# The first layer's shift on TensorE, and v's weights split ahead of h's parts, in a four-layer float32 kernel

## The reference

```
c_act = silu(c)                                   # (1, 1024)
mod = c_act @ w_mod[0] + b_mod[0]                 # (1, 6 * 1024)
sh_a, sc_a, gt_a, sh_f, sc_f, gt_f = split(mod, 6)
h = rmsnorm(x, g_mix_pre[0]) * (1 + sc_a) + sh_a  # (1, 256, 1024)
qkv = h @ w_qkv[0]                                # v first, then q and k
```

## Time and profile before

| what | value |
|---|---|
| median of 3 runs | 1455.71 us (1454.94 to 1458.83) |
| the profiled execution | 1458.6 us, span of its core 1457.4 us |
| PE busy | 1347.1 us, 92% of the span |
| DVE busy | 1051.8 us, 72% |
| ACT busy | 741.6 us, 51% |
| read from memory | 313.32 MB |

### The profile page before, as it was taken

The page is one execution under the profiler, slowest core; times in us unless marked ns, Lnnn a source line. Parts: engine busy times, 40 slices in busy tenths (PEclk is TensorE's granted clock), DMA queues, the critical chain, the costliest instruction groups (busy, mean ns, idle before and its releaser), DMA issues.

```text
span 1457.4 us, 22183 instructions
## 1 busy us (share of the span) xinstructions
PE 1347.1 (92%) x8848; PEld 1206.4 (83%) x8848; DVE 1051.8 (72%) x1628; ACT 741.6 (51%) x1241; POOL 104.3 (7%) x146
## 2 busy tenths in 40 slices
PE   4899899999899989999858999889999999899999
PEld 3798799987688779997646777579998899799987
DVE  6777788887648778789755675767878697666643
ACT  3665755543746575453634555564444454644441
POOL 0012000000004100000022241200000000000000
PEclk9999999999999999999988999989999999999999
DMA  8865467779467534667730512338788657356550
GB/s 339 333 231 209 167 241 257 283 310 340 146 218 272 200 119 174 242 249 279 272 141 30 202 58 109 123 118 306 297 316 309 243 218 273 127 221 238 224 202 29
DMA packets 46758, 315.81 MB, mean 217 GB/s; under 512 B 5168, under 2 KB 7744, under 8 KB 9280
## 3 DMA queue, kind: packets, MB, share of 16 engines
q1 hardware_dynamic: 46656, 314.40, 57.4%
HBM read 313.32 MB, written 1.06 MB: 216 GB/s over the span
## 4 chain that ended last, share of the span: by engine, by line
PE 64%; DVE 16%; ACT 7%; DMA 6%; issue 4%; POOL 2%; SPq 1%; DVEq 0%; ACTq 0%; POOLq 0%
PE mat L578 13%; PE mat L580 13%; PE mat L579 13%; DVE wlo L1470 6%; PE mat L617 5%; PE mat L619 5%; PE mat L621 5%; DVE raw L1488 3%; ACT whi L1038 3%; DMA raw<-in_down 2%; DMA raw<-in_mod 1%; POOL st L2058 1%; PE mat L930 1%; ACT tmp L1061 1%; DMA raw<-in_qkv 1%
## 5 line engine op out<-in xcount | busy, mean ns | idle before, releaser
L1470 DVE TENSOR_TENSOR wlo<-raw,whi 128x1024 fp32r<-128x1024 f32 x393 | 475.9, 1227 | 195.3 <-ACT whi L1038 194.1
L578 PE MATMUL mat<-hHL,whi 128*128 128x256 f32 x1864 | 534.0, 287 | 7.4 <-DVE tmp L1691 3.3
L579 PE MATMUL mat<-hHL,whi 128*128 128x256 f32 x1864 | 530.1, 284 | 0.0
L580 PE MATMUL mat<-hHL,wlo 128*128 128x256 f32 x1864 | 529.9, 284 | 0.0
L1038 ACT ACTIVATE whi<-raw 128x1024 fp32r<-128x1024 f32 x393 | 405.7, 1052 | 229.2 <-DMA raw<-in_down 75.9
L578 PEld LDWEIGHTS mat<-hHL,whi 128*128 128x128 f32 x1864 | 359.4, 193 | 14.1 <-issue 5.3
L579 PEld LDWEIGHTS mat<-hHL,whi 128*128 128x128 f32 x1864 | 359.5, 193 | 0.1
L580 PEld LDWEIGHTS mat<-hHL,wlo 128*128 128x128 f32 x1864 | 359.2, 193 | 0.0
L1488 DVE SCALAR_TENSOR_TENSOR raw<-raw,cB 128x1024 f32<-128x1024 f32 x192 | 233.9, 1229 | 13.7 <-DMA raw<-in_mod 13.5
L617 PE MATMUL mat<-whi,aHL 128*128 128x512 f32 x352 | 114.1, 394 | 2.1 <-DVE wlo L1470 2.0
L619 PE MATMUL mat<-wlo,aHL 128*128 128x512 f32 x352 | 112.9, 391 | 0.0
(11 more groups left out here) (207 smaller groups left out, 1539.4 us busy)
## 6 DMA issues: line engine op xcount, KB each, us to landing
raw<-in_mod SPq DMA_DIRECT2D x96, 1024.0 KB, 5.6
raw<-in_qkv SPq DMA_DIRECT2D x48, 1024.0 KB, 7.0
raw<-in_gate SPq DMA_DIRECT2D x44, 1024.0 KB, 5.0
raw<-in_up SPq DMA_DIRECT2D x44, 1024.0 KB, 5.3
raw<-in_down SPq DMA_DIRECT2D x44, 1024.0 KB, 5.8
raw<-in_wo SPq DMA_DIRECT2D x16, 1024.0 KB, 4.9
cB<-in_crow SPq DMA_DIRECT2D x3, 512.0 KB, 8.6
x<-in_x SPq DMA_DIRECT2D x1, 1024.0 KB, 8.9
```

Source lines behind the costliest of these rows:

```text
L578: pe.matmul(o, wh[:, k, :], hH[:, k, :], start=(k == 0), stop=False)
L579: pe.matmul(o, wh[:, k, :], hL[:, k, :], start=False, stop=False)
L580: m = pe.matmul(o, wl[:, k, :], hH[:, k, :], start=False, stop=(k == KT - 1))
L1470: dve.tensor_tensor(out=wlo[:, n % NSPL, :], in0=raw[:, f % NRAW, 1024 * h:1024 * h + 1024], in1=whi[:, n % NSPL, :].bitcast(f32), op=ALU. ...
```

## The change

Three quarters of the shift (q = 1 to 3) leave DVE. Their weights are laid out on the host with the summed index on the partitions, and `silu(c)` is also kept as a column of 128 partitions x 8 (`ccol`); TensorE makes 16 products of one column each for a quarter, with the 128x128 weights as the loaded operand, plain float32, into bank 4 of PSUM (`start_shift(q)`). Quarter 1 is put before v's first product, quarter 2 after group 1 and quarter 3 after group 3. The fetch four places on now waits for these products (`s_shift`). In each round ACT splits both halves of v's weights (`hi(2)`) before it makes h, and DVE both (`lo(2)`) before the two pieces of `hL`. The column's `silu` is put on ACT between the two squares of x.

```diff
-STEPS_FIRST = [(0, p, j) for q in range(4) for p in (1, 0) for j in (2 * q, 2 * q + 1)]
+STEPS_FIRST = [(0, 1, 0), (0, 1, 1), (0, 0, 0), (0, 0, 1)] + [(0, 1, j) for j in range(2, 8)]
...
+                    if old[:3] == ("mod", 0, 0) and old[3] > 0:
+                        sp.wait_ge(s_shift, old[3])
...
+        def start_shift(q):
+            f = FETCH_OF["mod", 0, 0, q]
+            w = raw[:, f % NRAW, :].rearrange("p (k n) -> p k n", k=8)
+            if q == 1:
+                pe.wait_ge(s_ccol, 1)
+                pe.wait_ge(s_tma, 2)
+            else:
+                pe.wait_ge(s_mod, FIN_AT[0, 1, q - 1])
+            pe.wait_ge(s_raw[f % NRAW], 16 * (f // NRAW + 1))
+            for i in range(2):
+                for k in range(KT):
+                    m = pe.matmul(shift_tile(q)[:, i:i + 1], w[:, k, P * i:P * i + P], ccol[:, k:k + 1], start=(k == 0),
+                                  stop=(k == KT - 1))
+            m.then_inc(s_shift, 1)
...
+            start_shift(1)
...
-                          then={(0, 0): lambda: transposes(b, 0, 2, 3), (5, 0): lambda: by_tile_second(b)} if l else None)
+                          then={(0, 0): lambda: transposes(b, 0, 2, 3), (5, 0): lambda: by_tile_second(b)} if l else
+                          {(1, 1): lambda: start_shift(2), (3, 1): lambda: start_shift(3)})
...
+                if t == 0:
+                    act.wait_ge(s_small, 16)
+                    act.activation(ccol[:, :], sm[:, SM["c"][0]:SM["c"][0] + 8], ACT.Silu).then_inc(s_ccol, 1)
             act.wait_ge(s_tr, 2)
...
+            for q in range(4):
+                hi(2)
+                for k in (2 * q, 2 * q + 1):
+                    y = start_rows(k)
+                    if k % 2 == 0:
+                        act.wait_ge(s_mod, FIN_AT[0, 1, q])
...
+            if q:
+                dve.wait_ge(s_shift, q)
+            dve.tensor_tensor(out=modc[:, 0, at], in0=shift_tile(q) if q else modc[:, 0, at], in1=sm[:, b[0]:b[0] + 2], op=ALU.add).then_inc(s_mod, 1)
...
             for q in range(4):
-                for p, j in ((1, 2 * q), (1, 2 * q + 1), (0, 2 * q), (0, 2 * q + 1)):
-                    mod_step(0, p, j)
...
+                for j in (2 * q, 2 * q + 1):
+                    mod_step(0, 1, j)
...
                 start_columns(q)
+                lo(2)
                 for k in (2 * q, 2 * q + 1):
-                    lo(1)
```

More of the change, by code:

```diff
@@ L23, in _layout @@
             [(f"wc{l}{k}", FT) for l in range(2) for k in range(3)] + [(f"bc{l}", FT) for l in range(2)] + \
-            [(f"sc{k}", 8) for k in range(3)] + [("bf", 1)]:
+            [(f"sc{k}", 8) for k in range(3)] + [("bf", 1), ("c", 8)]:
         SM[name] = (at, n)
@@ L162, in _mod_counts @@
             if (l, p) in ((0, 0), (0, 1)):
-                if p == 0 and j % 2:
+                if p == 1 and j % 2:
                     FIN_AT[0, 1, j // 2] = 3 * (j // 2) + 3
@@ L237, in build @@
         sm = sb("sm", [P, NSM])
+        ccol = sb("ccol", [P, KT])
         modc = sb("modc", [P, 26, 8])
@@ L261, in build @@
             "s_half", "s_prod", "s_tile", "s_tr", "s_trc", "s_gate_row"))
-        s_mem, s_const, s_c = (sem(n) for n in ("s_mem", "s_const", "s_c"))
+        s_mem, s_const, s_c, s_ccol, s_shift = (sem(n) for n in ("s_mem", "s_const", "s_c", "s_ccol", "s_shift"))
         s_hi, s_lo, s_tma, s_tmd, s_hh, s_hl = (sem(n) for n in ("s_hi", "s_lo", "s_tma", "s_tmd", "s_hh", "s_hl"))
@@ L506, in sync_program @@
                     old = FETCHES[f - NRAW]
-                    if old[0] == "w":
+                    if old[:3] == ("mod", 0, 0) and old[3] > 0:
+                        sp.wait_ge(s_shift, old[3])
+                    elif old[0] == "w":
                         sp.wait_ge(s_lo, CHUNKS[old[1]][2][-1] + 1)
@@ L665, in start_tile, with shift_tile @@
             return bank(4 + k // 2)[:, 256 * (k % 2):256 * (k % 2) + 256]
+        def shift_tile(q):
+            return bank(4)[:, 2 * q:2 * q + 2]
+        def start_shift(q):
[12 more added lines that the diff above has]
+            m.then_inc(s_shift, 1)
         def tensor_program():
@@ L1168, in scalar_program @@
                 act.activation(xn[:, t, :], x[:, t, :], ACT.Square, accum_out=norm_sum(0, t, 1)).then_inc(s_sq, 1)
+                if t == 0:
+                    act.wait_ge(s_small, 16)
+                    act.activation(ccol[:, :], sm[:, SM["c"][0]:SM["c"][0] + 8], ACT.Silu).then_inc(s_ccol, 1)
             act.wait_ge(s_tr, 2)
[L1170 to L1178, removed]
+            for q in range(4):
[4 more added lines that the diff above has]
+                        act.wait_ge(s_mod, FIN_AT[0, 1, q])
+                    act.activation(y, start_tile(k), ACT.Identity, bias=modc[:, 0, k:k + 1], scale=modc[:, 1, k:k + 1]
+                                   ).then_inc(s_tma, 1)
+                    act.wait_ge(s_tma, k + 1)
+                    act.activation(hH[:, k, :], y, ACT.Copy).then_inc(s_hh, 1)
             for l in range(LAYERS):
@@ L1515, in start_columns @@
             b, g = ([SM[name][0] + 2 * q for name in names] for names in (("b00", "b01"), ("g0a",)))
-            dve.wait_ge(s_step, STEP_AT[0, 0, 2 * q + 1, 0])
-            dve.tensor_tensor(out=modc[:, 0, at], in0=modc[:, 0, at], in1=sm[:, b[0]:b[0] + 2], op=ALU.add).then_inc(s_mod, 1)
+            dve.wait_ge(s_step, STEP_AT[0, 1, 2 * q + 1, 0] if q else STEP_AT[0, 0, 1, 0])
             dve.tensor_tensor(out=modc[:, 1, at], in0=modc[:, 1, at], in1=sm[:, b[1]:b[1] + 2], op=ALU.add).then_inc(s_mod, 1)
-            dve.wait_ge(s_mod, 3 * q + 2)
+            dve.wait_ge(s_mod, 3 * q + 1)
             dve.scalar_tensor_tensor(out=modc[:, 1, at], in0=modc[:, 1, at], scalar=1.0, in1=sm[:, g[0]:g[0] + 2], op0=ALU.add,
                                      op1=ALU.mult).then_inc(s_mod, 1)
+            if q:
+                dve.wait_ge(s_shift, q)
+            dve.tensor_tensor(out=modc[:, 0, at], in0=shift_tile(q) if q else modc[:, 0, at], in1=sm[:, b[0]:b[0] + 2], op=ALU.add).then_inc(s_mod, 1)
         def head_mods(l, step):
@@ L1646, in vector_program @@
             for q in range(4):
-                for p, j in ((1, 2 * q), (1, 2 * q + 1), (0, 2 * q), (0, 2 * q + 1)):
-                    mod_step(0, p, j)
[L1649 to L1652, removed]
+                for j in (2 * q, 2 * q + 1):
+                    mod_step(0, 1, j)
+                if q == 0:
+                    for t in range(2):
+                        vector_start_scale(t)
+                    dve.wait_ge(s_small, 16)
+                    for j in range(2):
+                        mod_step(0, 0, j)
                 start_columns(q)
+                lo(2)
                 for k in (2 * q, 2 * q + 1):
-                    lo(1)
                     dve.wait_ge(s_hh, k + 1)
@@ L2103 @@
         arrays[f"mod{l}"] = np.concatenate([tok(mod[:, 1024 * p:1024 * p + 1024].T) for p in range(6)])
+        if l == 0:
+            arrays["mod0"][1:4] = mod[:, 256:1024].reshape(8, P, 3, 256).transpose(2, 1, 0, 3).reshape(3, P, 2048)
         if b == 0:
@@ L2141 @@
     parts["bf"] = bf
+    parts["c"] = I["c"][0]
     arrays["smalls"] = np.ascontiguousarray(np.concatenate([cols(parts[n]) for n in SM], axis=1))
```

## The result

The changed kernel takes 1463.69 us (median of 5, 1462.62 to 1468.04) against 1455.67 us of the kernel before: a ratio of 1.0052, 95% interval 1.0036 to 1.0067. It is slower by 0.5%, where 1448.5 was forecast.

A forecast was written before the change was run, and what follows sets the result against it. TensorE was taken to bound most of the kernel, the start's v product running at DVE's pace; with the first q product 7.2 earlier, 1455.7 - 7.2 = 1448.5 us, range 1444.5 to 1455.

The forecast's parts named there:

- The start of the q product as the measure: What the first 58 us lose or gain, the end does; the first q product starts at 57.93 before the change.
- the removal on DVE: Six mod_steps leave DVE, 6.9 us; a round then takes 6.2 against 9.9 if nothing is waited for.
- hidden by 1 us: Fetch of the first TensorE shift's weights lands at 19 to 20, under the second h's end at 20.9.
- The later fetches: Weights for the second and third shifts land with margins of 1.3 and 2; if late, about 1451.
- The shift's products: One-column products on TensorE: 0.11 each at the high clock, 0.205 at the low; 16 cost 1.75 or 3.3.
- my own formula: v's queue on TensorE ends at 43.7 + 64c, c being one shift product at the high clock; 0.11 gives 50.7.
- the slower rival: Each of the 48 shift products is loaded and passed several times: c = 0.44, 1469.6, slower from c = 0.222; 5%.
- Load and product in turn: A shift product's load and pass on TensorE don't overlap: c 0.19 to 0.30, 1.2 slower, 1457; 13%.
- The clock falls again: Thin shifts count as pauses, low clock follows on TensorE: 3 to 6 of the 7.2 lost, about 1452.5; 12%.
- the 50.5 of the queue: Sum along TensorE's queue from the first shift to the first q product: 50.5 against 57.93, 7.4 less.
- The rule of the Trainium skill: Read as a plain float32 product passing TensorE's array four times: c would be 4 x 0.11.

The follow-up runs named there:

- experiment 3: The changed kernel with every second term of the shift's sums in quarters 1 to 3 left out, 8 products instead of 16 a quarter: 1452.72 us, ratio 0.9962.
- experiment 5: The kernel of experiment 4 with shift products on ready rounded operands, one load-and-pass pair each, so sums of other data: 1448.03 us, ratio 0.996 to the kernel before.
- experiment 4: The changed kernel with silu(c)'s column repeated 128 times in each shift product, same loads: 1454.86 us, ratio 0.9984 to the kernel before.
- experiment 1: The kernel before with only the splitting of v's weights put ahead on ScalarE and VectorE, the shift staying on VectorE: 1451.01 us, ratio 0.9955.
- experiment 7: The kernel before with only the splitting ahead, as in experiment 1, measured a second time: 1450.69 us, ratio 0.9966.

## Why the prediction was wrong

**What held.** The start of the q product as the measure held (table). So did the removal on DVE: its steps, splits and pieces took what they were put at, and it waited for TensorE, not the other way. The first shift began at 20.95, put at 20.9, but that is luck: the second h, which I had put at 20.9, was over at 20.29, and it was the fetch that ended the wait, landing at 20.82 where I had put it at 19 to 20 and called it hidden by 1 us. The later fetches cost nothing. ACT's new order cost nothing that shows.

**The step that failed: "The shift's products".** I put one at 0.11 at the high clock and 0.205 at the low. It took 3.46 / 16 = 0.22 and, from start to start, 6.82 / 16 = 0.43. The reading was of line 816, "of which two take 0.22": two rows of the trace, not two products of the program. Line 816 has 32 rows, and the program issues it once for each of 16 heads. A plain float32 product is two load-and-pass pairs here, each 0.11. The transposes have one row each, 16 for 16, so their 0.205 was a load's price and not a plain product's. Experiments 3 and 5 show both: half the products cost half, and one-pair products cost 1.75 for a shift. By my own formula c = 0.22 gives 43.7 + 14.1 = 57.8, which is no gain at all, and just the break-even that I had named for the slower rival. That rival had the mechanism, several loads for one product, at twice the price. "Load and product in turn" had a c of 0.19 to 0.30, and 0.22 lies in it, but its mechanism is not what happened: 128 columns cost no more than one (experiment 4), and a product of one pair takes 0.11 (experiment 5). (The middle of its ends, 55.9 and 62.9, is 59.4 and not 59.1; its 1457 stands.)

**The rival that came true beside it.** "The clock falls again" had 12% and 3 to 6 us of price. It fell at the end of the second shift and behind the third, and cost, against the terms of my sum, 2.95 in groups 2 and 3 (8.35 instead of 5.4) and 1.8 in the last four (12.6 instead of 10.8), 4.75 in all. Experiment 4 shows that the single column was the reason. The argument against it, that a shift of 1.75 is shorter than those pauses, hung on the wrong price: at 3.5 to 3.9 it is longer than the 2.5 that had let the clock fall before, and at 1.7, in experiment 3, it didn't fall. I had priced the rivals one at a time, and one made the other.

**The sum again, with the measured terms**, against the 50.5 of the queue: first shift +3.5 (6.8 instead of 3.3), groups 0 and 1 +0.5 (7.1 instead of 6.6), second shift +2.2 (3.9 instead of 1.75, of which 0.4 is the clock's), groups 2 and 3 +2.95, third shift +1.7, the last four groups +1.8: 12.7, which makes 63.2.

**The rule of the Trainium skill.** The Trainium skill, "TensorE: Matmul & The Clock Gate", section "Terms", says of the transpose mode that it is four times faster for float32. I had multiplied line 816's 0.11 by that four, and 0.11 is one row of two: hence 0.44 and 1469.6, where 0.22 was measured. Between the transposes and the plain products the rows show 0.205 against 0.43 at the low clock, a factor of 2.1, and the measurement decides. As I had read it, four passes for a plain product, the factor nearly shows with more columns. The kernel before has plain float32 products of 256 columns too, line 815, again two rows for one product, and products of rounded parts with 256 columns, line 578, one row each. Two pieces of its chain, and line 815's rows:

```profile
58.45 0.12 PE mat L578
...
91.81 0.43 PE mat L815 x2
...
L815 PE MATMUL mat<-att,tri_neg x32: 379/380/483, 80.1 to 148.0; 128*128 128x256 f32 x32
```

With 256 columns the plain product takes 0.43 against 0.12, 3.6 times as long. With one column or 128 it takes 0.22 against the 0.11 of one pair in experiment 5, twice as long.

**Where the forecast of the whole went astray.** The gain that I gave to both halves of the change together belongs to one. The splitting ahead alone brings the q product forward by 5.6. Taking the shift off DVE could add little: at the prices that I had forecast, with the clock's late rise (experiment 5), the first q product comes at 51.92, only 0.45 before the 52.37 of the splitting alone. At the real prices TensorE needs 21.6 for v's 96 products, and the three shifts of 3.5 to 6.8 in the same queue take 14.2 more.

**Open.** The medians are 8.0 apart where the q product's start says 5.3 and the spans 5.0. The interval (5.2 to 9.8 us) just holds 5.3; that executions of the kernel before differed by 12 us among themselves (1448.56 to 1460.94 in one comparison) may be all of it, and was not followed up. The span of a single execution is no witness: experiment 4's is 1447.9, 9.5 under that of the kernel before, where its q product says 2.1. Nor is it settled why the clock rose later in experiment 5 (at about 28) than in experiment 4 (inside the first shift, before 26.74), with 128 columns in both. And no run tells why a plain float32 product takes two pairs, only that it does.

## What to carry to other kernels

Before a price is read off a row, count the rows of that line against the instructions of the program: where there are twice as many, the instruction costs two rows. Work moved to TensorE as products of one column is paid for by its loads and can be paid again in the clock of the dense products behind it, so price the two together. Where a change has two halves, ask of each what it would do alone: here one line of order on ScalarE and VectorE held the gain, and the other half cost it.

## What was not expected of the hardware

- A plain float32 product with 128x128 loaded showed as two pairs of 0.109 us (3.48 us for 32 rows) at the high clock and 0.213 at the low (6.82 for 32), with one column and with 128 alike.
- Shifts of 3.5 to 3.9 us of one-column products, with PE and PEld busy throughout, were followed by the low clock, and one of 6.8 us did not end the low clock in which it began. With 128 columns the same products ended it within the first shift, and no fall followed the others.
- Pauses of 2.3 us in experiment 1 were followed by a fall one time of two, and so were the like ones in experiment 7. The stretches of experiment 1:

```profile
34.90:37.20 2.30, 0.05 (x1) 0.02 (x1) 2.30 (x4) 1.45 (x4) 0.00 (x0) 1.00 1.01 417
...
43.00:45.20 2.20, 0.00 (x1) 0.03 (x1) 2.20 (x4) 1.33 (x4) 0.00 (x0) 1.00 1.02 413
...
47.00:50.00 3.00, 3.00 (x8) 2.33 (x8) 1.15 (x2) 2.00 (x2) 0.00 (x0) 0.52 1.04 431
```

The first two are the pauses ahead of group 4 and ahead of group 6; behind the first the products ran at the high clock, two in 0.45, behind the second 0.52 was granted.

- The record of the granted clock can be wrong at the start of a run. In experiment 4 it says 1.00 from the first us on, yet in the first shift 15 rows take 3.20, the 0.213 each of the low clock:

```profile
21.30:24.50 3.20, 3.20 (x15) 3.20 (x16) 2.79 (x7) 0.89 (x1) 0.00 (x0) 1.00 0.99 410
```

So the level is read there from the length of the rows.
